# The start of a decoder step: two weight tiles per chunk of x, squares and low parts shared with GpSimd

## What is computed

```
h = x * rsqrt(mean(x * x) + 1e-6) * g_mix          # first norm, x is 280 tokens x 2048
q, k, v, glu, gate_a, gate_c = split(h @ w_in)     # 2048 x 9216
... stick-breaking attention, convolution branch, two branch projections, gates, output projection ...
x = x + peer_ffn(rmsnorm(x, g_ffn))                # expert mixer, most of the time
y = rmsnorm(x, g_final)
```

## Time and profile before

| | |
|---|---|
| median of 3 runs | 2192.7 us (2192.02 to 2192.89) |
| profiled execution | 2193.96 us |
| its span, first to last instruction | 2192.2 us |
| TensorE busy | 2171.4 us, 99% |
| VectorE, ScalarE, GpSimd busy | 1655.8, 1216.3 and 684.4 us |
| mean granted TensorE clock | 0.997 |

### The profile page before, as it was taken

How to read it: one execution, slowest core, us unless ns; L and a number is a source line. 1 busy time by engine, 2 the same in 40 slices (tenths; PEclk the granted TensorE clock), 3 DMA queues, 4 the chain that set the end, 5 groups by cost and what they waited for, 6 DMA issues and landing times.

```text
span 2192.2 us, 55777 instructions
## 1 busy us (share of the span) xinstructions
PE 2171.4 (99%) x16562; PEld 2131.2 (97%) x16562; DVE 1655.8 (76%) x3037; ACT 1216.3 (55%) x2220; POOL 684.4 (31%) x516
## 2 busy tenths in 40 slices
PE   9999999999999999999999999999999999999998
PEld 8999899999999999999999999999999999999997
DVE  8788788887766767888885444476678888888887
ACT  6445366667455445555555454444565565666664
POOL 0321100002011000788888888400255222111120
PEclk9999999999999999999999999999999999999999
DMA  7887766666556555777777887698789998888885
GB/s 244 285 294 245 248 196 213 215 227 212 181 187 205 177 169 181 187 179 187 187 180 175 201 185 182 158 336 281 234 278 325 331 339 314 281 296 295 299 284 188
DMA packets 337995, 514.37 MB, mean 235 GB/s; under 512 B 87277, under 2 KB 126565, under 8 KB 337773
## 3 DMA queue, kind: packets, MB, share of 16 engines
q1 hardware_dynamic: 263244, 427.59, 59.9%
q0 software_dynamic: 58016, 71.54, 13.0%
q10 hardware_dynamic: 16640, 14.16, 2.2%
HBM read 487.87 MB, written 25.24 MB: 234 GB/s over the span
## 4 chain that ended last, share of the span: by engine, by line
PE 76%; DVE 1%; DMA 0%; ACT 0%; issue 0%; DVEq 0%; SPq 0%; ACTq 0%
PE ps L2188 19%; PE ps L313 15%; PE ps L316 15%; PE ps L312 15%; PE ps L2194 10%; DMA raw<-weights 0%; PE ps L1395 0%; PE ps L2175 0%; DVE x L2164 0%; ACT hi L295 0%; PE ps L2216 0%; DVE lo L300 0%; DVEq L2219 0%; DVE x L2105 0%; DVE work L384 0%
## 5 line engine op out<-in xcount | busy, mean ns | idle before, releaser
L300 DVE TENSOR_TENSOR lo<-raw,hi 128x512 fp32r<-128x512 f32 x1504 | 1026.6, 694 | 459.6 <-ACT hi L295 432.8
L295 ACT CAST hi<-raw 128x512 fp32r<-128x512 f32 x1504 | 924.3, 620 | 710.4 <-PE ps L316 436.1
L312 PE MATMUL ps<-h_hi,hi 128*128 128x264 f32 (+1 forms) x3200 | 821.8, 286 | 1.9 <-DVE h_lo L955 1.9
L313 PE MATMUL ps<-h_lo,hi 128*128 128x264 f32 (+1 forms) x3200 | 820.2, 286 | 0.0
L312 PEld LDWEIGHTS ps<-h_hi,hi 128*128 128x128 f32 x3200 | 601.8, 188 | 8.7 <-issue 5.9
L313 PEld LDWEIGHTS ps<-h_lo,hi 128*128 128x128 f32 x3200 | 602.0, 188 | 0.3 <-issue 0.2
L316 PE MATMUL ps<-h_hi,lo 128*128 128x264 f32 (+1 forms) x3200 | 523.4, 285 | 2.1 <-DVE lo L300 2.0
L1742 POOL DMA_INDIRECT w_spill<-chosen,widx x256 | 437.7, 1710 | 266.0 <-DVE widx L1967 186.8
L2188 PE MATMUL ps<-whl,hi 128*128 128x432 f32 x2048 | 493.7, 361 | 0.5 <-DVE whl L2045 0.5
L316 PEld LDWEIGHTS ps<-h_hi,lo 128*128 128x128 f32 x3200 | 444.3, 188 | 3.8 <-DVE lo L300 3.6
L2188 PEld LDWEIGHTS ps<-whl,hi 128*128 128x128 f32 x2048 | 348.3, 190 | 8.8 <-DVE whl L2045 0.8
(11 more groups left out here) (299 smaller groups left out, 1712.8 us busy)
## 6 DMA issues: line engine op xcount, KB each, us to landing
raw<-u_tiles SPq DMA_DIRECT2D x512, 256.0 KB, 2.9
raw<-expert_v SPq DMA_DIRECT2D x512, 256.0 KB, 5.9
raw<-weights SPq DMA_DIRECT2D x480, 256.0 KB, 3.4
w_spill<-zeros ACTq DMA_DIRECT2D x16, 864.0 KB, 6.0
wld<-w_spill SPq DMA_DIRECT2D x32, 432.0 KB, 4.3
qb<-q_spill POOLq DMA_DIRECT2D x8, 512.0 KB, 5.9
w_spill<-chosen,widx POOLq DMA_INDIRECT x256
u_spill<-ust SPq DMA_DIRECT2D x128, 24.0 KB
```

The costliest lines, as they stand in the source:

```text
L295: nc.scalar.copy(hi[k % SPLIT][:], raw_quarter(k)).then_inc(hi_done, 1)
L300: nc.vector.tensor_tensor(lo[k % SPLIT][:], raw_quarter(k), hi[k % SPLIT][:].bitcast(F32), ALU.subtract).then_inc(lo_done, 1)
L312: pe.matmul(out, a, rhs[0][:, first + j, 0:n], start=start and j == 0, stop=False)
L313: pe.matmul(out, a, rhs[1][:, first + j, 0:n], start=False, stop=False)
```

## The change

The SP queue loads x's first chunk in two pieces of two K tiles, and puts two weight quarters behind each chunk, one of tile 0 and one of tile 1. TensorE multiplies tile 0 and tile 1 in turns, chunk by chunk, into banks 0 and 1, and waits within tile 0's quarter for each K tile's low part. The warm-up has four products. The 16 squares are shared: 8 ScalarE, 4 VectorE, the last 4 GpSimd; the three additions move into the loop. The sum product goes from behind quarter 10 to behind quarter 12 (`LATER` = 5). The norm's 16 steps stand without a gap, and its low parts are made by GpSimd.

```diff
--- before.py
+++ after.py
@@ -304,10 +304,12 @@
 
         eng.wait_ge(mm_done, 8 * i + 4 * b + 4 + SPLIT)
 
-    def quarter_products(pe, q0, k, out, rhs, first, n, start, stop):
+    def quarter_products(pe, q0, k, out, rhs, first, n, start, stop, ready=None):
 
         pe.wait_ge(hi_done, q0 + k + 2 * RAW + 1)
         for j in range(QT):
+            if ready is not None:
+                pe.wait_ge(ready, first + j + 1)
             a = hi[k % SPLIT][:, j]
             pe.matmul(out, a, rhs[0][:, first + j, 0:n], start=start and j == 0, stop=False)
             pe.matmul(out, a, rhs[1][:, first + j, 0:n], start=False, stop=False)
@@ -406,7 +408,7 @@
     gain_in, vec_in, const_ready = sem("gain_in"), sem("vec_in"), sem("const_ready")
     raw_h_hi, raw_h_lo = sem("raw_h_hi"), sem("raw_h_lo")
     fill0, glu_done = sem("fill0"), sem("glu_done")
-    x_sq_dve = sem("x_sq_dve")
+    x_sq_dve, x_sq_pool = sem("x_sq_dve"), sem("x_sq_pool")
     x_sq, x_sum, st_free, st_new = sem("x_sq"), sem("x_sum"), sem("st_free"), sem("st_new")
     rows_ready, part_ready, out_done, kv_done = sem("rows_ready"), sem("part_ready"), sem("out_done"), sem("kv_done")
     conv_done, tap_done = sem("conv_done"), sem("tap_done")
@@ -428,8 +430,8 @@
     NG = HEADS // GH
     NP = DEC * PAGES
 
-    NORM_AT = [1, 2, 3, 4, 5, 7, 8, 9, 10, 11, 13, 14, 15, 16, 17, 18]
-    LATER = 3
+    NORM_AT = list(range(1, KD + 1))
+    LATER = 5
 
     def norm_at(step):
 
@@ -493,15 +495,20 @@
         @block.sync
         def _(sp):
             def first_quarter(n):
-                s, r = n // 2, n % 2
-                sp.dma_start(raw[:, s, QT * r:QT * r + QT].rearrange("p a b -> p (a b)"),
-                             a_halves[s][:, QT * P * r:QT * P * (r + 1)]).then_inc(raw_in[s][r], 16)
+                s, b = n // 2, n % 2
+                h, r = 2 * b + s // 2, s % 2
+                sp.dma_start(raw[:, s, QT * b:QT * b + QT].rearrange("p a b -> p (a b)"),
+                             a_halves[h][:, QT * P * r:QT * P * (r + 1)]).then_inc(raw_in[s][b], 16)
+
             sp.dma_start(gain[:], gains).then_inc(gain_in, 16)
-            for c in range(4):
+            sp.dma_start(x[:, 0:2], xT[:, 0:2]).then_inc(gain_in, 16)
+            first_quarter(0)
+            sp.dma_start(x[:, 2:QT], xT[:, 2:QT]).then_inc(x_in[0], 16)
+            first_quarter(1)
+            for c in range(1, 4):
                 sp.dma_start(x[:, QT * c:QT * c + QT], xT[:, QT * c:QT * c + QT]).then_inc(x_in[c], 16)
-                first_quarter(c)
-            for n in range(4, 2 * RAW):
-                first_quarter(n)
+                first_quarter(2 * c)
+                first_quarter(2 * c + 1)
             for t, src in ((dw, w_dwT), (cvec, conv_vecs), (bias, sb_bias), (pages, page_table)):
                 sp.dma_start(t[:], src).then_inc(vec_in, 16)
             sp.dma_start(st[:, 0:KC * DEC * PADC], stateT.rearrange("p j b t -> p (j b t)")).then_inc(vec_in, 16)
@@ -553,6 +560,14 @@
                            allow_small_or_imprecise_dtypes=True).then_inc(const_ready, 1)
             nc.gpsimd.iota(part[:], pattern=[[0, 2]], base=0, channel_multiplier=1,
                            allow_small_or_imprecise_dtypes=True).then_inc(part_ready, 1)
+
+            for j in range(3 * QT, KD):
+                pool.wait_ge(x_in[j // QT], 16)
+                nc.gpsimd.tensor_tensor(sqs[:, j, :], x[:, j, :], x[:, j, :], ALU.mult).then_inc(x_sq_pool, 1)
+            for j in range(KD):
+                pool.wait_ge(norm_hi, j + 1)
+                nc.gpsimd.tensor_tensor(h[1][:, j, 0:NT], work[:, j % 4, 0:NT], h[0][:, j, 0:NT].bitcast(F32),
+                                        ALU.subtract).then_inc(norm_lo, 1)
 
             pool.wait_ge(rows_ready, 1)
             pool.wait_ge(tile_free[0], PAIR_Q + 1)
@@ -622,17 +637,20 @@
 
             act.wait_ge(fill0, 3)
             nc.scalar.activation(root[:, 0:2], eps[:], ACT.Copy, scale=1.0)
-            act.wait_ge(gain_in, 16)
+            act.wait_ge(gain_in, 32)
 
             def x_square(j):
                 nc.scalar.square(sqs[:, j, :], x[:, j, :]).then_inc(x_sq, 1)
             for c in range(4):
-                act.wait_ge(x_in[c], 16)
                 for j in range(QT * c, QT * c + QT):
+                    if j >= 2:
+                        act.wait_ge(x_in[c], 16)
                     nc.scalar.activation(h2[0][:, j, :], x[:, j, 0:LIVE], ACT.Copy, scale=gain[:, 0, j:j + 1])\
                         .then_inc(raw_h_hi, 1)
-                if c < AHEAD:
-                    split_hi(act, 0, c)
+                    if j % QT == 1:
+                        split_hi(act, 0, 2 * c)
+                if c < 3:
+                    split_hi(act, 0, 2 * c + 1)
 
             def copy_out(b):
                 def f(i):
@@ -691,14 +709,12 @@
                 act.wait_ge(t_added, 2 * (g + 1))
                 nc.scalar.activation(e[:], z[:], ACT.Exp).then_inc(a_ready, 1)
 
-            for k in range(4):
-                split_hi(act, 0, AHEAD + k)
-                for j in range(3 * k, 3 * k + 3):
-                    x_square(j)
             for t in range(1, 2 * PAIR_Q):
                 for k in range(4):
                     step = 4 * (t - 2) + k - LATER
                     split_hi(act, 8 * (t // 2), 4 * (t % 2) + AHEAD + k)
+                    for j in range(3 * k, min(3 * k + 3, 2 * QT) if t == 1 else 0):
+                        x_square(j)
                     if step == 0:
                         act_root(act, root, 1, D, 0, NT)
                     j = norm_at(step - 1)
@@ -788,19 +804,22 @@
             pe.sem_inc(o_done, 1)
             pe.sem_inc(mm_done, SPLIT)
             pe.wait_ge(fill0, 3)
-            for _ in range(5):
+            for _ in range(4):
                 pe.matmul(ps[:, 6, :].rearrange("p (a b) -> p a b", a=4), ones[:], spread(ones[:], 1, 4),
                           start=True, stop=True)
-            pe_tile_follow(pe, 0, 0, h2, LIVE, raw_h_lo, 0)
-            pe_tile(pe, 0, 1, h2, LIVE)
+            for r in range(4):
+                for b in range(2):
+                    quarter_products(pe, 0, 2 * r + b, ps[:, b, 0:LIVE], h2, QT * r, LIVE, r == 0, r == 3,
+                                     None if b else raw_h_lo)
             for r in range(4):
                 quarter_products(pe, 8, r, ps[:, 2, 0:LIVE], h2, QT * r, LIVE, r == 0, r == 3)
-                if r == LATER - 1:
+            for r in range(4):
+                quarter_products(pe, 8, 4 + r, ps[:, 3, 0:LIVE], h2, QT * r, LIVE, r == 0, r == 3)
+                if 4 + r == LATER - 1:
                     pe.wait_ge(x_sum, 3)
                     for j in range(QT):
                         m = pe.matmul(ps[:, 7, 0:NT], ones[:], sqs[:, j, :], start=j == 0, stop=j == QT - 1)
                     m.then_inc(sum_ready, 1)
-            pe_tile(pe, 1, 1, h2, LIVE, 3)
             pe_pairs(pe, 2, PAIR_Q, h2, LIVE)
             pe.wait_ge(tile_free[0], PAIR_Q + 1)
             pe_tile_follow(pe, PAIR_Q, 0, h, NT, norm_lo, 0)
@@ -947,44 +966,49 @@
         def _(dve):
             dve.sem_inc(lo_done, 2 * RAW)
             dve.sem_inc(glu_done, 1)
-            dve.wait_ge(gain_in, 16)
+            dve.wait_ge(gain_in, 32)
             for c in range(4):
-                dve.wait_ge(x_in[c], 16)
                 for j in range(QT * c, QT * c + QT):
+                    if j >= 2:
+                        dve.wait_ge(x_in[c], 16)
                     dve.wait_ge(raw_h_hi, j + 1)
                     nc.vector.scalar_tensor_tensor(out=h2[1][:, j, :], in0=x[:, j, 0:LIVE], scalar=gain[:, 0, j:j + 1],
                                                    in1=h2[0][:, j, :].bitcast(F32), op0=ALU.mult,
                                                    op1=ALU.subtract).then_inc(raw_h_lo, 1)
-                if c < AHEAD:
-                    split_lo(dve, 0, c)
+                    if j % QT == 1:
+                        split_lo(dve, 0, 2 * c)
+                if c < 3:
+                    split_lo(dve, 0, 2 * c + 1)
 
             def q_out(t):
-                tile_done(dve, t // 2, t % 2)
+                tile_done(dve, t // 2, t % 2 if t > 1 else 1)
                 bank = t if t < 4 else t % 2
                 nc.vector.scalar_tensor_tensor(out=qkv[:, t, 0:LIVE], in0=ps[:, bank, 0:LIVE], scalar=HD ** -0.5,
                                                in1=rstd[:, 0:LIVE], op0=ALU.mult, op1=ALU.mult)\
                     .then_inc(tile_free[t % 2], 1)
 
             def add_squares(into, more, squares, sums):
-                dve.wait_ge(x_sq, squares)
+                if squares:
+                    dve.wait_ge(x_sq, squares)
                 if sums:
                     dve.wait_ge(x_sum, sums)
                 nc.vector.tensor_tensor(sqs[:, into:into + QT, :], sqs[:, into:into + QT, :],
                                         sqs[:, more:more + QT, :], ALU.add).then_inc(x_sum, 1)
-            for k in range(4):
```

(21 more changed lines are left out.)

## The result

| | before | after |
|---|---|---|
| median (range) of 11 executions each, same chips | 2192.91 (2192.02 to 2194.63) | 2197.39 (2196.19 to 2199.76) |
| profiled execution | 2193.96 | 2196.49 |
| its span | 2192.2 | 2194.4 |

The ratio is 1.002, with a 95% interval of 1.0012 to 1.0027. The kernel became slower by 4.5 us where +1.8 was forecast, and 2197.39 lies 0.4 us above the range.

The account below looks back on a forecast made before the run. TensorE, busy for 2171.4 of 2192.2 us, was taken as the bound, with gains possible only in the first 30 us. Front -0.1 plus norm steps +1.9 gave +1.8 us, 2194.5 us; range 2190.8 to 2197.0.

Parts of the forecast that it names:

- The new feed: First 30 us: last chunk of x lands at 14.7 us, quarter 8 starts at 20.4 against 23.04, 2.6 us won.
- VectorE's sums: Squares and additions ahead of low part 11 make TensorE wait 1.8 us in quarter 11, 0.9 with contention.
- GpSimd beside VectorE: Each new GpSimd instruction costs a busy VectorE 0.58 us; the four squares cost 2.3 us when the last chunk lands.
- whole block: Rival, chance 0.09: each GpSimd instruction costs VectorE its full 0.80 us; +6.2 us, 2198.9 us.
- no contention: Rival, chance 0.22: the engines meet seldom or GpSimd slips into VectorE's waits; -0.8 us, 2191.9 us.
- The norm steps: 16 steps of 1.69 us against TensorE's 1.46: 3.7 us behind, less 1.8 in hand; TensorE waits 1.9 us, quarters 28 to 34.
- Later nothing is late: Behind the norm steps: K and V tiles need h only at quarter 35, page loads wait for later events; nothing added.
- front: Start of the kernel up to quarter 12: gain of the new feed less sums and GpSimd squares, net -0.1 us.
- the forecast's band: Contention at a price of 0.5 to 0.65 us per GpSimd instruction: -0.1 to +3.3 us, chance 0.56.

Follow-up runs that it names:

- no_gpsimd: The kernel after with neither squares nor low parts on GpSimd (ScalarE makes 12 squares, VectorE 4 and the low parts): 2194.74 us, +1.3 to its before.
- spread_sums: The kernel after with GpSimd squaring the first chunk, VectorE the last four, the three additions at three places, the norm's low parts on VectorE: 2191.02 us, -2.2 to before.
- q_by_sync: The kernel after with the write of the query moved from GpSimd's queue to SP's, between two weight quarters: 2193.30 us, 0.0 to its before.
- low_on_vector: The kernel after with the norm's 16 low parts back on VectorE, the four squares staying on GpSimd: 2194.08 us, +0.6 to its before.
- before_q_by_sync: The kernel before with the write of the query moved from GpSimd's queue to SP's: 2192.88 us, -0.4 to before.
- q_first: The kernel after with the query written ahead of GpSimd's memset of `kvbd`, right behind the page loads: 2196.66 us, +3.2 to its before.
- pages_early: The kernel after with VectorE making the page numbers two quarters earlier, ahead of the last low parts of q's stage: 2195.80 us, +2.6 to its before.
- extra_writes: `low_on_vector` with 16 GpSimd memsets of 264 columns into unused tiles where after has its 16 low parts: 2194.68 us in a single profiled execution.
- after_filled: The kernel after with two products of ones put into TensorE's list between the high and low products of quarter 47: 2196.54 us, +3.9 to its before.
- look2: The kernel after, unchanged, profiled once more: 2198.06 us.
- look1: The kernel after, unchanged, profiled once more: 2195.87 us.
- after_again: The kernel after, unchanged, measured again beside the second group: 2197.36 us, +4.2 to its before.

## Why the prediction was wrong

**The new feed: right.** The last chunk was put at 14.7 us, and GpSimd, which waits for it, starts at 14.64. Quarter 8 without contention was put at 20.4, `no_gpsimd` and `spread_sums` have it at 20.12 and 20.18. With contention I said 22.1 and the trace says 21.80; the GpSimd squares cost 1.7 us there, not 2.3.

**VectorE's sums: right.** A wait of 0.9 us (0.85 in the working) for low part 11 was forecast; quarter 11 lasts 2.28 us instead of 1.46, which is 0.82 more, and quarter 12 starts at 28.44 instead of 28.8. Without contention it is 2.02 us (1.8 forecast), and `spread_sums` removes it altogether by placing the additions apart.

**GpSimd beside VectorE: the price right, 0.60 for 0.58 us.** With the median of 1103 ns against 502, the rival "whole block" (0.80) and "no contention" are both out. For the four squares it was lower, 1.7 us in all, some 0.4 each (quarter 8 starts at 21.07 to 22.04 in the eleven profiles with these squares beside the last chunk, at 20.12 to 20.64 in the three without).

**The norm steps: over-sized.** Forecast 1.9 us of TensorE's waits, measured 0.5 (0.44 us ahead at quarter 17, 0.07 at quarter 32, 0.05 behind at quarter 35, 64.63 against 64.58). Two sizes were off. VectorE entered the steps with more in hand: low part 17 starts at 35.52 and is done at 36.20, and TensorE wants it at 38.59, which leaves 2.4 us, not 1.8. Of the 0.6 between, 0.2 are the longer quarter behind the sum product, which my 6.8 us left out. And a step took 1.64 us, not 1.69: from the first of these low parts to the last (VectorE in order of time)

```profile
35.52 0.68 DVE L300 TENSOR_TENSOR lo<-raw,hi 128x512 fp32r<-128x512 f32 x1
...
61.74 0.68 DVE L300 TENSOR_TENSOR lo<-raw,hi 128x512 fp32r<-128x512 f32 x1
```

16 steps take 26.22 us. Over 16 steps 0.05 us are 0.8; with 0.6 more in hand 0.5 of the 1.9 are left, as measured. At quarter 32 the kernel was therefore 0.07 us ahead where my sum said 1.8 behind. I had said that a start below 59.9 at quarter 32 would prove me wrong; it was 59.88.

**The step that failed:** "Later nothing is late: K and V tiles need the last of h only at quarter 35, and GpSimd's page loads wait for later events." The page loads wait for the page numbers, and VectorE makes these at the end of the very backlog that I had worked out: 3.2 us late. I asked how long TensorE would wait for low parts, found it small in the steps, and took the backlog for paid. But VectorE's list goes on behind it, with one item that another engine turns into a chain of four links (gather, query out, query broadcast, product), and a weight's low part stands behind the end of that chain. `q_by_sync` and `low_on_vector` cut the chain at two different places. Each removes the stall, and their medians are 0.0 and 0.6 us over their before instead of 4.5.

So the sum went: front -0.44 (forecast -0.1), norm steps +0.49 (+1.9), page chain +1.97 (0), together +2.0 at quarter 48 (85.55 before, 87.57 after) and 2.06 at L918; 0.3 us are added outside the span (1.76 us before, 2.09 after). With 0.1 in the rest of the span that is the 2.5 us of the two profiles. Against `before_q_by_sync`, whose start is the same as before's, the front gain is nothing (quarter 17 at 37.63 and 37.62) and L918 is 2.5 us late; so the front is known to about 0.4 us only. Two terms of chance, before's profile above its median (1.05) and after's below (0.90, likely the executions with a clock fall), make up the 4.5 of the medians by arithmetic; that these are their causes was not shown. By its own slope (2 us for each 0.1 us of price) the forecast's band for a price of 0.50 to 0.65 is +0.2 to +3.2, not -0.1 to +3.3; the range does not hang on that.

Had the page chain not been touched, the answer would have been about that of `low_on_vector` or `q_by_sync`, "same", as forecast. That the forecast's +1.8 is near the 2.06 us of the traces is luck: 1.4 too much in the norm steps and 0.3 of front gain too little stand against 2.0 left out in the page chain.

**Open.** Why the time outside the span is 2.1 us in after, `q_first`, `pages_early` and `extra_writes`, 2.6 in `after_filled`, and 1.7 to 1.8 in before and the others was not tested. Why the medians differ by 4.5 us where the traces show 2.1 to 2.5 is explained only in part. Nor was it tested what decides whether the clock falls after a stall.

## What to carry to other kernels

When an engine is found to run behind for a stretch, don't stop at the engine that waits for it there: go down its list behind the stretch, and for each item that releases another engine follow that chain to its end, with the room it has in the trace of before. A small DMA that ends a long chain should not stand in a queue behind large ones; one moved issue undid the whole loss here. An engine taken in as a helper costs the helped one what they contend for: count 0.6 us a meeting here against the 0.36 us that each moved low part had cost.

## What the runs showed of the hardware

- GpSimd's subtractions, which read SBUF, lengthen VectorE's two-input scalings from 502 to 1103 ns (median, after); 16 memsets beside two-input instructions lengthen none (0.50 and 0.68 us, `extra_writes`).
- A 32 KB write issued on GpSimd's queue right behind page loads landed after 7.9 us; issued 2.75 us later, after 5.2 us; so at the same moment. On SP's queue it had landed 4.9 us after its issue.
- A stall of TensorE can cost more than its length: after 2.26 us in `look2` and 2.02 us in `no_gpsimd` the granted clock was 0.50 for some microseconds; after 2.11 us in `look1` and 2.06 us in `after_again` it stayed at 1.00.
